# First block of a two-block transformer step on one Trainium2 core: its projections from float32 to three float32r passes, with attention units moved and the gates' sigmoids batched

## The reference

```python
h = rmsnorm(x, norm_mix_g)
proj = h @ w_in                                   # 1024 x 7424 columns
qkv_a, q_b, k_b, v_b, gate_logits = jnp.split(proj, split_at, axis=-1)
...                                               # branch a: 3 groups x 8 heads, dilated windows
...                                               # branch b: 8 query heads on 2 key/value heads
gates = jax.nn.sigmoid(gate_logits.reshape(b, s, N_BRANCHES, d) + b_gate)
merged = gates[:, :, 0] * (o_a @ w_proj_a) + gates[:, :, 1] * (o_b @ w_proj_b)
x = x + (merged @ w_out).astype(x.dtype)
h2 = rmsnorm(x, norm_ffn_g).reshape(b * s, d)
ff = moe_ffn(h2, w_router, b_router, w_gate_up, b_gate_up, w_down, b_down)   # top 4 of 32 experts
x = x + ff.reshape(b, s, d).astype(x.dtype)
```

## Time and profile before

| what | value |
|---|---|
| median of three runs | 2214.77 us |
| the profiled execution, its own time | 2213.98 us |
| its span, first to last instruction | 2212.2 us |
| mean granted TensorE clock, share of full | 0.966 |
| TensorE busy (products) | 2065.7 us, 93% |
| VectorE busy | 973.3 us, 44% |
| ScalarE busy | 301.0 us, 14% |
| GpSimd busy | 88.3 us, 4% |
| read from HBM | 558.21 MB, mean 253 GB/s |

### The profile page before, as it was taken

How to read it: one execution, slowest core, us unless ns; L and a number is a source line. 1 busy time by engine, 2 the same in 40 slices (tenths; PEclk the granted TensorE clock), 3 DMA queues, 4 the chain that set the end, 5 groups by cost and what they waited for, 6 DMA issues and landing times.

```text
span 2212.2 us, 24206 instructions
## 1 busy us (share of the span) xinstructions
PE 2065.7 (93%) x9832; PEld 1240.5 (56%) x9832; DVE 973.3 (44%) x1570; ACT 301.0 (14%) x526; POOL 88.3 (4%) x107
## 2 busy tenths in 40 slices
PE   7989999999999999999999999997869997988997
PEld 4444664544444444444444347866858885766885
DVE  3321333422333333333222334646657676667765
ACT  1112440111011011110010012211100000211000
POOL 1210000000000000000000000104200000000000
PEclk9988999899999999999999999998989998999998
DMA  9423123599999999999999994430225444424551
GB/s 361 151 76 114 47 81 132 229 424 427 428 428 428 427 428 428 428 428 428 428 428 428 427 428 172 147 119 1 77 76 188 155 174 164 157 76 171 171 200 48
DMA packets 106013, 560.13 MB, mean 253 GB/s; under 512 B 5856, under 2 KB 11232, under 8 KB 81248
## 3 DMA queue, kind: packets, MB, share of 16 engines
q1 hardware_dynamic: 102528, 551.61, 62.1%
q10 hardware_dynamic: 3424, 7.67, 1.0%
HBM read 558.21 MB, written 1.05 MB: 253 GB/s over the span
## 4 chain that ended last, share of the span: by engine, by line
PE 69%; DMA 19%; DVE 7%; issue 2%; POOL 1%; ACT 1%; SPq 0%; POOLq 0%; DVEq 0%; ACTq 0%
DMA ring<-in_w_gate_up_dram 18%; PE ps L954 13%; PE ps L711 12%; PE ps L993 7%; PE ps L994 7%; PE ps L995 7%; PE ps L980 5%; PE ps L929 3%; PE ps L1042 2%; PE ps L917 2%; PE ps L1050 1%; PE ps L747 1%; PE ps L1122 1%; PE ps L780 1%; PE ps L1136 1%
## 5 line engine op out<-in xcount | busy, mean ns | idle before, releaser
L954 PE MATMUL ps<-ring,arena 128*64 128x512 f32 x2048 | 451.2, 596 | 8.9 <-DMA ring<-in_w_gate_up_dram 8.9
L954 PEld LDWEIGHTS ps<-ring,arena 128*64 128x64 f32 x2048 | 142.9, 137 | 301.0 <-issue 276.9
L711 PE MATMUL ps<-ring,actT 128*128 128x512 f32 (+1 forms) x544 | 245.1, 605 | 1.9 <-DMA ring<-in_w_in_dram 1.8
L1992 DVE TENSOR_SCALAR arena<-ps 128x512 f32<-128x512 f32 x32 | 22.1, 692 | 505.1 <-PE ps L954 505.1
L993 PE MATMUL ps<-split_w,act_parts 128*128 128x512 f32 (+1 forms) x544 | 215.7, 397 | 26.7 <-DVE act_parts L1609 26.7
L980 PE MATMUL ps<-ring,arena 128*64 128x512 f32 x1024 | 226.8, 595 | 0.0
L994 PE MATMUL ps<-split_w,act_parts 128*128 128x512 f32 (+1 forms) x544 | 211.0, 388 | 0.0
L995 PE MATMUL ps<-split_w,act_parts 128*128 128x512 f32 (+1 forms) x544 | 210.7, 387 | 0.0
L1609 DVE TENSOR_TENSOR split_w<-ring,split_w 128x2048 fp32r<-128x2048 f32 (+2 forms) x92 | 198.1, 2153 | 3.2
L711 PEld LDWEIGHTS ps<-ring,actT 128*128 128x128 f32 x544 | 104.8, 198 | 123.6 <-issue 120.0
L980 PEld LDWEIGHTS ps<-ring,arena 128*64 128x64 f32 x1024 | 70.7, 137 | 133.3 <-issue 133.3
(11 more groups left out here) (299 smaller groups left out, 2113.7 us busy)
## 6 DMA issues: line engine op xcount, KB each, us to landing
ring<-in_w_gate_up_dram SPq DMA_DIRECT2D x128, 2048.0 KB, 21.9
ring<-in_w_down_dram SPq DMA_DIRECT2D x64, 2048.0 KB, 19.8
ring<-in_f_w_dram SPq DMA_DIRECT2D x28, 2048.0 KB, 7.9
ring<-in_w_in_dram SPq DMA_DIRECT2D x14, 2048.0 KB, 10.2
ring<-in_a_w_in_dram SPq DMA_DIRECT2D x8, 2048.0 KB, 7.8
ring<-in_b_w_qkv_dram SPq DMA_DIRECT2D x6, 2048.0 KB, 8.0
ring<-in_f_w_dram SPq DMA_DIRECT2D x4, 1536.0 KB, 6.9
ring<-in_w_out_dram SPq DMA_DIRECT2D x2, 2048.0 KB, 8.4
```

Of the source, the lines that this page charges most:

```text
L711: mm = pe.matmul(ps[:, bank, 0:n], lhs(k), slot_ap[:, k, :], start=(k == 0), stop=(k == kn - 1))
L954: mm = pe.matmul(ps[half, bank, :], xeT[:, 2 * c + j, :], w[:, j, at:at + 512], start=False, stop=(c == 3 and j == 1), skip_group_check=True)
```

## The change

- The chunks 2 to 14, both branch projections and the output projection are done as three float32r passes. Chunks 0 and 1 stay float32.
- Each of these loads is split in four quarters of 1024 elements a partition: ScalarE casts the high part (`cast_quarter`), VectorE subtracts for the low part (`low_quarter`). A chunk's quarters are made during the chunk before it, one at each half. The raw weights now use two slots (1 and 0; load 2 has slot 4), and the parts lie in the memory of the slots 2 to 5; a raw load waits for the quarters of two loads before (`pre_split`).
- The inputs, the attention's outputs and the merged rows are also split in a high part by ScalarE and a low part by VectorE.
- The attention steps move: three each at the chunks 8 and 9, four at 10, one behind each half of 11 to 14.
- The gates' sigmoids are taken behind the attention, four of 1024 elements, with the casts of the second branch projection between them. The gates' bias is loaded in four pieces.
- The branch projections run with b outside, all four groups of a branch in a row. The output projection runs n outside, tile inside.
- The first expert's chunks 0 and 1 are loaded once the output projection's raw halves are split, 2 and 3 once its first two groups are done, 4 and 5 once all four are.
- The split of the experts' biases moves behind the first `hot_rows`; some semaphores in the expert loop are merged.

```diff
+            for half in range(2):
+                events.append(("half", c, tile, half))
+                if half and c - (tile == 0) in HEAD_CHUNKS and (c, tile) != (0, 0):
+                    events.append(("turn_heads", c - (tile == 0), 1 - tile))
+                if c >= 11 or c in (8, 9) and (tile, half) != (0, 0) or c == 10:
+                    events.append(("attend", step))
+                    step += 1
...
+def raw_slot(load):
+    return (1, 0, 4)[load] if load < 3 else (1, 0)[(load - 3) % 2]
...
+def quarter_at(c, tile, half):
+    if c < 2:
+        return [(2, q) for q, at in enumerate([(0, 1, 0), (0, 1, 1), (1, 0, 0), (1, 0, 1)])
+                if at == (c, tile, half)]
+    return [(c + 1, 2 * tile + half)]
...
+                if i >= 3:
+                    if i < 5:
+                        sync.wait_ge(gemm_ready, 2 * (i - 3) + 2)
+                    else:
+                        sync.wait_ge(pre_split, quarters_done(i - 2, 3))
...
+                if c < 2:
+                    sync.wait_ge(pre_split, quarters_done(OUT_LOAD + c, 3))
+                else:
+                    sync.wait_ge(gemm_ready, G_OUT + c // 2 * 2)
...
+                        if k % (kn // 4) == 0:
+                            pe.wait_ge(pre_split, quarters_done(load, k // (kn // 4)))
+                        mm = exact(dst, parts(k),
+                                   [part_place(load, i, kn, LOAD_N[load])[:, k, at:at + n]
+                                    for i in range(2)], **edge)
...
+            def cast_quarter(load, q):
+                kn, n = LOAD_K[load], LOAD_N[load]
+                if q == 0:
+                    act.wait_ge(loaded[raw_slot(load)], 16 * (loads_into(raw_slot(load), load) + 1))
+                    if load == 3:
+                        act.wait_ge(pre_split, quarters_done(2, 3))
+                    elif load == OUT_LOAD:
+                        act.wait_ge(gemm_ready, G_PROJ + 4)
+                    elif load == OUT_LOAD + 1:
+                        act.wait_ge(gemm_ready, G_PROJ + 8)
+                    elif load > 3:
+                        act.wait_ge(gemm_ready, 2 * (load - 2) + 2)
+                s_ = slice(kn // 4 * q, kn // 4 * q + kn // 4)
+                act.activation(part_place(load, 0, kn, n)[:, s_, :],
+                               slot(raw_slot(load), kn, n)[:, s_, :], ACT.Copy).then_inc(pre_cast, 1)
...
             for event in TIMELINE:
+                if event[0] == "half":
+                    for load, q in quarter_at(*event[1:]):
+                        cast_quarter(load, q)
...
-                        s = gates[:, tile, group * 512:(group + 1) * 512]
-                        act.activation(s, s, ACT.Sigmoid).then_inc(gates_ready, 1)
+                        if tile and group < 3:
+                            act.dma_start(gate_rows, everyone("b_gate", 512 * group + 512, 512))\
+                                .then_inc(bias_in, 16)
...
+            for g in range(G_PROJ - 3, G_PROJ):
+                read_out(act, g)
+            for tile in range(NT):
+                gate_sigmoid(tile, 0)
+                for q in range(2 * tile, 2 * tile + 2):
+                    cast_quarter(PROJ_LOAD + 1, q)
+            for tile in range(NT):
+                gate_sigmoid(tile, 1)
+            for q in range(4):
+                cast_quarter(OUT_LOAD, q)
...
+            def low_quarter(load, q):
+                kn, n = LOAD_K[load], LOAD_N[load]
+                s_ = slice(kn // 4 * q, kn // 4 * q + kn // 4)
+                dve.wait_ge(pre_cast, quarters_done(load, q))
+                dve.tensor_tensor(part_place(load, 1, kn, n)[:, s_, :],
+                                  slot(raw_slot(load), kn, n)[:, s_, :],
+                                  part_place(load, 0, kn, n)[:, s_, :], ALU.subtract)\
+                    .then_inc(pre_split, 1)
...
             for event in TIMELINE:
+                if event[0] == "half":
+                    for load, q in quarter_at(*event[1:]):
+                        low_quarter(load, q)
...
+            for q in range(2):
+                low_quarter(PROJ_LOAD + 1, q)
+            for i in range(4):
+                tile, n = divmod(i, 2)
+                g = G_PROJ + i
+                dve.wait_ge(gates_ready, tile + 1)
+                if n:
+                    low_quarter(PROJ_LOAD + 1, 2 + tile)
+                dve.wait_ge(gemm_ready, g + 1)
+                dve.tensor_tensor(merged[:, tile, n * 512:(n + 1) * 512], ps[:, g % GB, :],
+                                  gates[:, tile, D + n * 512:D + (n + 1) * 512], ALU.mult)\
+                    .then_inc(gemm_free[g % GB], 1)
+            for i in range(4):
...
+                low_quarter(OUT_LOAD, i)
```

More of the change, by code:

```diff
@@ L166, with loads_into, quarters_done @@
 G_MOE = G_OUT + 4
+LOAD_K = [KD] * PROJ_LOAD + [4, 4, KD, KD]
+LOAD_N = [w[3] for w in W_CHUNKS] + [D, D, 512, 512]
+FULL_LOADS = 2
+def raw_slot(load):
+    return (1, 0, 4)[load] if load < 3 else (1, 0)[(load - 3) % 2]
+def loads_into(slot, load):
+    return len([i for i in range(load) if raw_slot(i) == slot])
+def quarters_done(load, quarter):
+    return 4 * (load - FULL_LOADS) + quarter + 1
+def quarter_at(c, tile, half):
[3 more added lines that the diff above has]
+    return [(c + 1, 2 * tile + half)]
 HD2 = 128
@@ L281, in slot_of @@
 def slot_of(chunk):
-    return (PRE_LOADS + chunk) % RING
+    return (1, 0, 4, 5, 2, 3)[chunk]
 def loads_before(slot):
-    return len(range(slot, PRE_LOADS, RING))
+    return loads_into(slot, PRE_LOADS)
 def program(nc, t, out):
@@ L702, in _, with exact, products @@
         def _(pe):
-            def products(g, lhs, slot_ap, k0, k1, kn, n, load, bank=None):
-                bank = g % GB
+            def exact(dst, left_parts, right_parts, start, stop):
+                (lh, ll), (rh, rl) = left_parts, right_parts
+                pe.matmul(dst, lh, rh, start=start, stop=False)
+                pe.matmul(dst, lh, rl, start=False, stop=False)
+                return pe.matmul(dst, ll, rh, start=False, stop=stop)
+            def products(g, load, lhs, parts, k0, k1, at, n):
+                bank, kn, slot_ = g % GB, LOAD_K[load], raw_slot(load)
                 if k0 == 0:
@@ L1590, in after, with turn_out @@
                 dve.wait_ge(v_step, n)
-            def turn_out(first, tile, gain):
+            def turn_out(first, tile, gain, into=actT):
                 for b in range(2):
@@ L1671, in _ @@
             after(tables)
+            for tile in range(NT):
+                for b in range(2):
+                    s_ = (slice(None), slice(4 * b, 4 * b + 4), slice(tile * P, (tile + 1) * P))
+                    dve.wait_ge(act_high_done, 2 * tile + b + 1)
+                    dve.tensor_tensor(pre_low[s_], xT[s_], pre_high[s_], ALU.subtract)\
+                        .then_inc(x_split, 1)
             inverted = {}
@@ L1826, in residual @@
             def residual(tile, n):
-                g = G_OUT + 2 * tile + n
+                g = G_OUT + 2 * n + tile
                 dst = res[:, tile, n * 512:(n + 1) * 512]
@@ L1979, in _ @@
             hot_rows(1)
+            dve.wait_ge(raw_bias_in, 64)
+            c = step.on(dve.tensor_copy(bias_parts[:, :, :], raw_bias))
+            after(c)
+            for q in (1, 3):
+                low_rows = slice(NE * q, NE * q + NE)
+                ins = dve.tensor_tensor(bias_parts[low_rows], raw_bias[low_rows],
+                                        bias_parts[low_rows], ALU.subtract)
+            ins.then_inc(bias_split, 1)
             dve.wait_ge(m_gathered, 1)
```

235 lines of the change are left out of this document (114 added, 121 removed).

## The result

The changed kernel took 2164.65 us (median of four runs, 2164.42 to 2165.1), beside 2215.09 us for the kernel before (four runs, 2214.71 to 2216.74): ratio 0.9771, 95% interval 0.9754 to 0.9788. The profiled executions span 2163.0 and 2212.2 us, 49.2 apart. The forecast was 2163, range 2150 to 2182.

What follows compares the result with a forecast made beforehand. TensorE was taken to bound the changed stages (0 to 392 us), VectorE and an engine loop after the change. Gains of 39.5 us to the last scaling and 12.5 in the projections made 52 off 2212.2: median 2163, range 2150 to 2182.

Steps and rivals of the forecast that it cites:

- Start: Stage up to chunk 2: VectorE's added subtracts delay chunk 2 from 39.3 to 42.2, 2.9 us lost.
- Heads: Heads' projections, 12 groups: VectorE becomes the bound, period 7.14 us, TensorE idles 1.2; end 131.8, before 162.2.
- Most of which is not products: Heads' stage: most of the 30 us gain there comes from attention units leaving the stage, their work coming later.
- Values: Value chunks with 10 attention units: a ScalarE, VectorE, TensorE loop takes 5.42 us a unit, against 4.9 of TensorE work.
- Gates: Gate chunks: the loop paces slots at 6.53 us, 7.14 with a gate add; last scaling ends at 290.6, before 330.1.
- Sigmoids: Gate chunks: batching takes some 14 table loads off ScalarE; given no gain, though without it the loop would be longer.
- Projections behind: Branch and output projections after the attention: 49.4 us against 61.9 before, gain 12.5.
- The clock did not fall in the heads' stage: Rival, heads' stage: short TensorE waits lower the clock; 4 us (2167) to 43 us (2206); 15% something between, 3% full.
- The rival in which nothing but TensorE's work counts: Heads, value and gate chunks: VectorE and the loop do not pace them; 24 us more gain, 2138; 5%.
- The passes did not run at the lower clock: Rival: all float32r passes run at the lower clock, 0.43 us against 0.2265; 164 us more, 2327; 2%.
- no side fell out: Rival, only one side gives: late weights from chunk 8 on lose the split's gain behind the heads, 2184; 8%.
- Unchanged stages: Expert stage stays at 945 us; later expert loads, the moved bias split and merged semaphores are worth nothing.

Runs made afterwards that it cites:

- PSUM input: Kernel with low quarters in the power's wait and later transposes, with chunks 3 to 8 subtracting PSUM banks instead of the cast part (other numbers): 2148.69 us, ratio 0.9699.
- high part in PSUM: Changed kernel with low quarters moved, transposes later, and ScalarE copying chunks 3 to 8's cast quarters into PSUM for VectorE's subtract: 2146.20 us, ratio 0.9688.

## Why the prediction was right

The time, 2163 against 2164.65, and the sum, 52 us against 54.5 at the router's mark, came out. That the time fits to 1.65 us is in part luck: 2.5 us too little there stood against 5.3 that the profile shows lost behind it, where the forecast had nothing. Of the 5.3, 0.8 lie between the router and the first expert block, 2.1 in the expert loop and 2.4 behind it. The change touches these parts only by the first expert's later loads, the place of the bias split and merged semaphores, and in the second profile of the same kernel the loss is 2.5.

- **Start.** Chunk 2 forecast at 42.2, found at 41.2.
- **Heads.** Period forecast 7.14, found 7.11; end 131.8, found 131.7; TensorE's wait forecast 1.2, found 0.86; of the difference 0.15 is that a pass here took 0.233 us and not the 0.2265 of the earlier trace rows. That VectorE and not TensorE paces this stage was the step that mattered: with VectorE out of the way, in the runs with the PSUM input and the later transposes, it ended at 120. "Most of which is not products" was right: 28.0 of 30.5 us came with the move alone.
- **Casts and quarters.** Forecast 1.06 and 1.225, found 1.05 and 1.22.
- **Values.** Pair unit forecast 5.42, found 5.24.
- **Gates.** Slots forecast at 6.53 and 7.14, found 6.42 and 6.88. This is the mis-sized term: the loop's handovers were put too long by a quarter of a microsecond, and TensorE's own slot too short (6.2, found 6.41), so that of two slots in turn the one is TensorE's and only the other the loop's. TensorE's slot could have been had from the rows: the old 7.06, less a float32 half of 3.43, with 12 passes added, is 6.35 at 0.2265 us a pass and 6.43 at the 0.233 found. The outputs stood at 286.9 and not 290.6. (The sum of 16 slots is 109.4 us and not 108, which went into nothing further.)
- **Sigmoids.** I gave the batch nothing and added that without it the loop would be longer; the run without it shows 4.6 us, of which 0.5 was there before the gates.
- **Projections behind.** 49.4 forecast, 50.4 found; the output projection's 96 passes took 0.233 us and not 0.2265, 0.6 of that 1.0, while the branch projections' took 0.227.
- **Rivals.** The clock did not fall in the heads' stage: 1.00 through its 90.6 us, with a wait of TensorE in each period. The Trainium skill (TensorE: Matmul & The Clock Gate, "A second HAM failure mode: psum-queue depth-cycling") tells of a kernel in which frequent short idles between groups made the clock swing; here idles of 0.86 us every 7.1 us did not. Longer ones did in two of the edited kernels (3.4 us of the lower clock behind waits of 2.48 and 1.66 us) and not in a third (1.64 us). The rival in which nothing but TensorE's work counts (2138) was shut out by both engines' order; the run with the high part in PSUM shows how near one comes to it (2146) once that order and the contention are dealt with. The passes did not run at the lower clock, and no side fell out.
- **Unchanged stages.** Right on the whole. They carry a scatter of several microseconds, for which the sum had no term; the range covered it by the width that other terms gave.

## What to carry to other kernels

When a stage of products has an idle TensorE, look first for what the engine that serves it does in between: moving work of an in-order engine out of that stage gave 28 us here before any product was made cheaper, and the cheaper products gave 0.7 where that work had stayed. Before filling a wait of VectorE for GpSimd, look at the inputs of the filler: with two in SBUF 1.7 of its 2.35 us came back as a later GpSimd, with one of them in PSUM nothing did. And judge small edits by marks in the trace close behind the stage: these repeated to 0.9 us, and the length between two of them behind the start to 0.1, whereas the rest of the program scattered by 7.1. Where a sum of edits falls short, look at the granted clock of the stretch before naming a cause.

## What the hardware showed that I had not expected

- GpSimd's two small operations on 8 columns took 1.14 and 2.48 us beside VectorE's subtracts with two SBUF inputs, 0.24 and 1.66 beside the same subtract with one input in PSUM. VectorE's subtract took 1.22 and 1.21.
- A subtract that reads one input from PSUM is not slower than one that reads both from SBUF (1211 against 1217 ns for 1024 elements a partition).
- A float32r pass of 512 columns went by in 0.233 us with the first block's inputs or merged rows (`pre_high`, `pre_low`) and in 0.227 with the attention's outputs (`oT_parts`), at the same granted clock of 1.00. Why was not tried.
- The same kernel gets another clock from execution to execution, 0.85 and 1.00 in the same 20 us, though TensorE's wait ahead is 1.38 us in both. In two kernels with the same waits in the heads' stage (0.9 and 1.65 us) the clock stayed in one and fell for 3.4 us in the other, at a cost of 1.5 us.
